# The third FFN's output stage by weight rows, and a mixer that runs two blocks ahead instead of three

## The reference

```python
for i in range(DEPTH):                                     # 2 layers
    sh1, sc1, g1, sh2, sc2, g2, sh3, sc3, g3 = split(silu(c) @ ada_w[i] + ada_b[i], 9)
    x = x + 0.5 * g1 * swiglu_ffn(modulate(rms_norm(x), sh1, sc1), ffn_w_in[i, 0], ffn_w_out[i, 0])
    h = modulate(rms_norm(x), sh2, sc2)
    m = retention(h, ...) if i == 0 else s5_layer(h, ...)  # s5: diagonal scan, then GLU
    x = x + g2 * m
    x = x + 0.5 * g3 * swiglu_ffn(modulate(rms_norm(x), sh3, sc3), ffn_w_in[i, 1], ffn_w_out[i, 1])
return rms_norm(x)

# s5_layer: states = scan(A_bar, u @ B_bar); y = gelu(Re(C states) + d u)
#           y1, y2 = split(y @ w_glu, 2); return y1 * sigmoid(y2)
```

## Time and profile before

| | us |
|---|---|
| median of 3 runs | 2099.3 (2098.71 to 2100.33) |
| span of the profiled execution | 2097.0 |
| TensorE busy in it | 2042.8 (97%) |
| VectorE, ScalarE, GpSimd busy | 1156.3, 602.9, 46.1 |
| output stage of the third FFN | 1447.3 to 1567.0 |
| us_norm | 1567.0 to 1574.0 |
| mixer, first states to last outputs | 1574.0 to 1649.1 |

### The profile page before, as it was taken

The page is one execution under the profiler, slowest core; times in us unless marked ns, Lnnn a source line. Parts: engine busy times, 40 slices in busy tenths (PEclk is TensorE's granted clock), DMA queues, the critical chain, the costliest instruction groups (busy, mean ns, idle before and its releaser), DMA issues.

```text
span 2097.0 us, 26064 instructions
## 1 busy us (share of the span) xinstructions
PE 2042.8 (97%) x10343; PEld 1742.3 (83%) x10343; DVE 1156.3 (55%) x1653; ACT 602.9 (29%) x717; POOL 46.1 (2%) x55
## 2 busy tenths in 40 slices
PE   4999999999999999999999999999998999999998
PEld 3788888988888889888888988888887898888886
DVE  6677556655455436886544566654448664233322
ACT  2322222323323323222222322332332333222222
POOL 2000000000000000000000000000002000000000
PEclk9999999999999999999999999999999999999999
DMA  8465655433132143667545344545668323333221
GB/s 320 140 200 179 201 191 176 136 126 106 61 124 102 45 161 108 213 212 266 171 148 166 114 131 151 162 147 170 203 221 318 116 81 101 100 100 100 90 96 55
DMA packets 246574, 314.89 MB, mean 150 GB/s; under 512 B 31904, under 2 KB 219552, under 8 KB 244128
## 3 DMA queue, kind: packets, MB, share of 16 engines
q1 hardware_dynamic: 212432, 274.74, 39.9%
q10 hardware_dynamic: 34064, 39.07, 5.3%
HBM read 290.44 MB, written 27.53 MB: 152 GB/s over the span
## 4 chain that ended last, share of the span: by engine, by line
PE 60%; issue 32%; DVE 4%; DMA 2%; ACT 1%; POOL 0%; ACTq 0%; POOLq 0%; SPq 0%; DVEq 0%
PE ps L1784 14%; PE ps L1785 14%; PE ps L1786 14%; PE ps L1811 5%; PE ps L1812 5%; PE ps L1815 5%; DVE ada_first L976 1%; DMA sq<-y_dram 1%; PE ps L2070 1%; DMA csil<-in_c 0%; PE ps L2207 0%; DMA y_dram<-acc 0%; DMA tb<-s_lags 0%; PE ps L2061 0%; DVE w_lo L966 0%
## 5 line engine op out<-in xcount | busy, mean ns | idle before, releaser
L550 ACT ACTIVATE w_hi<-w_raw 128x1024 fp32r<-128x1024 f32 x352 | 345.9, 1029 | 350.3 <-PE ps L1786 241.0
L966 DVE TENSOR_TENSOR w_lo<-w_raw,w_hi 128x1024 fp32r<-128x1024 f32 x172 | 210.2, 1222 | 371.7 <-ACT w_hi L550 369.8
L1784 PE MATMUL ps<-g_hi,w_lo 128*128 128x512 f32 (+1 forms) x952 | 345.7, 363 | 0.0
L1786 PE MATMUL ps<-g_hi,w_hi 128*128 128x512 f32 (+1 forms) x952 | 344.9, 362 | 0.0
L1785 PE MATMUL ps<-g_lo,w_hi 128*128 128x512 f32 (+1 forms) x952 | 344.9, 362 | 0.0
L1784 PE MATMUL ps<-h_hi,w_lo 128*128 128x512 f32 x880 | 344.1, 391 | 0.3 <-DVE w_lo L966 0.3
L1786 PE MATMUL ps<-h_hi,w_hi 128*128 128x512 f32 x880 | 342.7, 389 | 0.0
L1785 PE MATMUL ps<-h_lo,w_hi 128*128 128x512 f32 x880 | 342.6, 389 | 0.0
L1811 PE MATMUL ps<-h_hi,w_lo 128*128 128x512 f32 x688 | 269.8, 392 | 2.0 <-DVE w_lo L966 2.0
L1812 PE MATMUL ps<-h_hi,w_hi 128*128 128x512 f32 x688 | 268.5, 390 | 0.0
L1815 PE MATMUL ps<-h_lo,w_hi 128*128 128x512 f32 x688 | 212.4, 390 | 0.0
(11 more groups left out here) (268 smaller groups left out, 2310.1 us busy)
## 6 DMA issues: line engine op xcount, KB each, us to landing
w_raw<-in_ffn_w_in SPq DMA_DIRECT2D x86, 1024.0 KB, 6.2
ada_raw<-in_ada_w SPq DMA_DIRECT2D x128, 512.0 KB, 4.6
w_raw<-in_ffn_w_out SPq DMA_DIRECT2D x32, 1024.0 KB, 6.7
w_raw<-in_ret_w_in SPq DMA_DIRECT2D x24, 1024.0 KB, 5.2
w_raw<-in_ffn_w_out SPq DMA_DIRECT2D x16, 768.0 KB, 4.5
tb<-s_rec ACTq DMA_DIRECT2D x8, 1536.0 KB, 12.5
w_raw<-in_ret_w_out SPq DMA_DIRECT2D x8, 1024.0 KB, 5.1
w_raw<-in_s_w_glu SPq DMA_DIRECT2D x8, 1024.0 KB, 6.2
```

Of the source, the lines that this page charges most:

```text
L550: copy = lambda o, i: nc.scalar.activation(o, i, ACT.Copy)
L966: V.tensor_tensor(w_lo[k % 2][:, 0:HALF, :], w_raw[k % 2][:, 0:HALF, :], raw_f32(w_hi[k % 2][:, 0:HALF, :]), ALU.subtract).then_inc(w_lo_h ...
L1784: nc.tensor.matmul(o, wl, xh, start=start, stop=False)
L1786: return nc.tensor.matmul(o, wh, xh, start=False, stop=stop)
```

## The change

The third FFN's output stage gets functions of its own, `out_by_rows`, on SyncE (written out in `ffn`), ScalarE, VectorE and TensorE. The order of its twelve chunks is now by weight rows: rows 0 to 7 for all four pairs, then rows 8 to 15, then the last six; the eight output tiles are summed in all eight PSUM banks. With that, g's first eight tiles are free after four chunks and the next eight after eight; tables 2 and 3, then 4 and 5, are moved to that space and loaded there during the stage (`tables_in`), tables 0 and 1 behind the second chunk. A modulation half goes with each of the first eight chunks. All residuals and hop stores are in the last four chunks. The last `us_load`s are issued at the start of the mixer. In the mixer states run two blocks ahead on two banks (`AHEAD`), tile 0 of the gelu output is used from block 2 on, a tile per block, and the low part of GLU chunk 1 is made earlier. GpSimd waits for the scans instead of the gelu tiles.

```diff
-V_BANK, Y_BANK = (0, 1, 2, 3, 0, 1, 0, 1), (4, 6, 7, 4, 6, 4, 6, 4)
-Y_HI = ((), (), (0,), (1, 2), (3,), (4,), (5,), (6,))
-Y_USED = ((), (), (), (0,), (1, 2), (3,), (4,), (5,))
+V_BANK, Y_BANK = (0, 1) * 4, (4, 6) * 4
+AHEAD = 2
+Y_HI = ((), (0,), (1,), (2,), (3,), (4,), (5,), (6,))
+Y_USED = ((), (), (0,), (1,), (2,), (3,), (4,), (5,))
...
-        tb += [sb(f"tb{2 + k}", [P, REC], F32, g_at + k * HB) for k in range(4)]
+        tb += [sb(f"tb{2 + k}", [P, REC], F32, (g_at, gl_at)[k % 2] + k // 2 * HB) for k in range(4)]
...
+                if f == 2:
+                    for at in range(len(FFN_OUT) * OUT_PAIRS):
+                        c, o = at // OUT_PAIRS, at % OUT_PAIRS
+                        load(n0 + 2 * FFN_PAIRS + at, at, ffn_out[f][:, 8 * c:8 * c + FFN_OUT[c], o * CW:(o + 1) * CW])
+                        if at < 2 * OUT_PAIRS:
+                            load_ada(a_out + at // 2, *q_of(a_out + at // 2), at % 2)
+                    return
...
-                    elif b < 6:
+                    else:
                         pool.wait_ge(sc_done, b - 2)
-                    else:
-                        pool.wait_ge(a5_lo, (1, 3)[b - 6])
...
+            def out_by_rows(n0, chunks, pair0):
+                for at in range(len(chunks) * OUT_PAIRS):
+                    c, o = at // OUT_PAIRS, at % OUT_PAIRS
+                    split_hi(n0 + at + 1, at + 1, chunks[(at + 1) // OUT_PAIRS % len(chunks)])
+                    if at == 1:
+                        first_tables()
+                    if at in (OUT_PAIRS, 2 * OUT_PAIRS):
+                        act.wait_ge(w_used, n0 + at + 1)
+                        tables_in((2 * c, 2 * c + 1))
+                    if c < len(chunks) - 1:
+                        continue
+                    if o:
+                        for t in range(2):
+                            us_load(2 * o - 2 + t)
+                    square(pair0 + o, 2 * o)
+                    if o == OUT_PAIRS - 1:
+                        split_hi(C_GLU + 1, 1)
+                    if o == 0:
+                        act.wait_ge(scale_u, 1)
+                    for t in range(2):
+                        u_tile(2 * o + t)
...
-                for r in range(2):
-                    act.wait_ge(u_out[r], 16 * KT // 2)
-                tables_in(range(2, 6))
+                for t in range(KT - 2, KT):
+                    us_load(t)
...
-                    if b == 0:
+                    if b == 1:
                         act.wait_ge(w_lo_done, C_GLU + 3)
                         tables_in(range(6, KT))
-                    if b == 1:
-                        for t in range(KT - 2, KT):
-                            us_load(t)
...
+                split_lo_half(C_GLU + 1, 1)
                 dve.wait_ge(rstd_done, k + 1)
...
-                split_lo_half(C_GLU + 1, 1)
+                split_lo_rest(C_GLU + 1, 1)
...
+            def out_by_rows(n0, chunks, pair0, ada):
+                for at in range(len(chunks) * OUT_PAIRS):
+                    c, o = at // OUT_PAIRS, at % OUT_PAIRS
+                    split_lo(n0 + at + 1, at + 1, chunks[(at + 1) // OUT_PAIRS % len(chunks)])
+                    if at < 2 * OUT_PAIRS:
+                        ada_half(ada + at // 2, at % 2)
+                    if c < len(chunks) - 1:
+                        continue
+                    pair = pair0 + o
+                    dve.wait_ge(tile_done, pair - TILES_LESS[pair0 // OUT_PAIRS])
+                    residual_of(2 * o, 2 * o).then_inc(x_half, 1)
...
+            def out_by_rows(n0, chunks, g_all):
+                pe.wait_ge(win_copied, KT)
+                pe.wait_ge(lag_copied, KT)
+                pe.wait_ge(skip_added, KT)
+                for c, r in enumerate(chunks):
+                    if c == len(chunks) - 1:
+                        pe.wait_ge(g_lo_done, g_all)
+                    for o in range(OUT_PAIRS):
+                        at = c * OUT_PAIRS + o
+                        if c == len(chunks) - 1:
+                            chunk_by_tile(n0 + at, at, g_hi, g_lo, 8 * c, r, 2 * o, False, tile_done)
+                        else:
+                            chunk(n0 + at, at, g_hi, g_lo, 8 * c, r, 2 * o, c == 0, False)
...
-                for b in range(3):
+                for b in range(AHEAD):
                     states(b)
                     chunk_outputs(b)
...
                     outputs(b)
-                    if b == 3:
+                    if b + AHEAD < KT:
+                        states(b + AHEAD)
+                    if b == AHEAD:
                         pe.wait_ge(w_lo_done, C_GLU + 3)
-                        pe.wait_ge(gelu_done, 3)
                     for done in Y_USED[b]:
                         first_glu(done)
-                    if b + 3 < KT:
-                        states(b + 3)
-                    if b < 2:
-                        chunk_outputs(b + 3)
-                    elif 3 <= b < KT - 2:
-                        chunk_outputs(b + 2)
+                    if b + AHEAD < KT:
+                        chunk_outputs(b + AHEAD)
```

106 lines of the change are left out of this document (56 added, 50 removed).

## The result

The changed kernel takes 2133.38 us (median of 4 runs, 2132.45 to 2135.55) where the kernel before takes 2099.01 (4 runs, 2097.84 to 2100.33): a ratio of 1.0167, 95% interval 1.0152 to 1.0181. The sign of the forecast was right and its size was not: +34.4 us instead of +23.0, and 2133.4 lies above the range of 2108 to 2130.

What follows compares the result with a forecast made beforehand. TensorE's own work was taken to bound the kernel, so only its waits could move the time. The stage's +27.0 us and the mixer's -4.0 gave +23.0 on 2099.3, so 2122.3 us, with a range of 2108 to 2130.

Steps and rivals of the forecast that it cites:

- The bound: Whole kernel: TensorE's work bounds it, so only its waits move time; stage has none to lose, mixer 9.5 us.
- The loading loop: Output stage, SyncE's queue: weights load singly, 13.9 us per loop against a turn of 10.9; stage loses 26.3 us.
- six waits: TensorE idle ahead of w_lo between 1480 and 1561: 3 us each, 6 to 8 at chunks 3 and 6, some 26.
- The bandwidth: Loads behind tables: 406 GB/s taken; at 358 GB/s two chunks land some 2 us later each, sum 4 us higher.
- The last four turns: End of output stage: VectorE's and ScalarE's work both under 8.2 us per turn, so no cost; 0.7 added for clock.
- The norm: Ahead of the mixer's first states: a 0.3 us delay from the earlier GLU low half, counted within the mixer's sum.
- The mixer: Waits fall from 11.2 to 7.0 us with the new order and early tables; gain 4 us, from 1.5 to 6.
- (c): Mixer gains nothing, as block 1's y travels with tables 6 and 7 and scans wait; 2126.3 us, chance 0.13.
- (a): Output stage: tables pass in the weight queue's pauses, chunks 3 and 6 after 13.9 us; 2111.9 us, chance 0.14.
- (b): Output stage: weights keep up, stage stays at 119.7 us, only the mixer's gain left; 2095.3 us, chance 0.06.
- (d): Effects cancel: larger lead and shorter landings, so the stage loses only 4 to 8 us; 2099 to 2103, chance 0.03.
- VectorE's gap of 4 us: Mixer: VectorE's long idle of 4.39 us, while ScalarE waited for block 0's y, was to be gone afterwards.

Runs made afterwards that it cites:

- E1: Changed kernel with each modulation half in SyncE's queue moved behind the next weight load; 2104.4 us, ratio 1.0026.
- e2: Changed kernel with VectorE doing each modulation half ahead of the split of the next chunk, SyncE's queue unchanged; 2105.5 us, ratio 1.0036.
- E7: E1 with ScalarE's last four turns reordered: high split, one hop copy, first square, other copy, second square; 2097.1 us, ratio 0.9990 to the kernel before.
- e11: Changed kernel with only E7's ScalarE order in the last four turns, SyncE's queue unchanged; 2128.3 us, ratio 1.0140.
- e8: E1 with all eight hop copies and their loads moved behind the stage's last square and last high split; 2106.8 us, one run.
- e6: New mixer alone: changed kernel with the earlier kernel's output stage and tables 2 to 5 loaded at the mixer's start; 2106.8 us, ratio 1.0043.
- E10: E7 with GpSimd's scaling for blocks 5 to 7 waiting for VectorE's low half of the gelu output; 2095.4 us, ratio 0.9986.
- e12: E7 with ScalarE's gelu high halves and the GLU products at their old, later blocks, states still two blocks ahead; 2094.5 us, ratio 0.9981.
- e13: e12 with GpSimd's multiply also waiting for VectorE's gelu low half, as in the kernel before; 2094.3 us, ratio 0.9978.

## Why the prediction was right in sign and short in size

**The bound.** That only TensorE's waits can move the time, and that the stage had none to lose, held but for the clock: 10343 matmuls in both, and all differences are waits or clock. Of the 36.2 us 14.1 are slower matmuls and 22.1 are waits, and the sum had priced the clock at 0.7.

**The loading loop** was right in mechanism. The chunks were forecast for 1486.3, 1500.2, 1514.1, 1533.2, 1547.1 and 1560.6 and came at 1486.3, 1501.2, 1516.1, 1534.3, 1548.9 and 1562.8. The period is 14.9 us instead of 13.9. The part from landing to next issue is 14.9 - 8.6 = 6.3 us (6.6 in the forecast), so the miss is the landing: 8.6 us where the nearest rows, 7.0 and 7.7, made me take 7.3. Chunk 3, behind tables 0 and 1, came to the tenth as forecast, because the landing was longer (13.2 instead of 12.5) and the steps around it shorter; the turn behind tables 2 and 3 took 18.2 us (1516.1 to 1534.3) instead of 19.1. In sum chunk 8 came 2.2 us later than forecast. E1 and e2 show the loop as the cause. I forecast six waits of 3 and 6 to 8 us; they are 1.8 to 6.7, 21.4 in sum, and the other 7 us up to chunk 8 are products at a low clock (0.92 in the window), which start TensorE's next turn later and so shorten its next wait. I had named that and counted it once, which came out right.

**The bandwidth.** A window of the kernel before, with the tables of the mixer under way, moves 427 GB/s, and the two landings behind tables, 13.2 and 11.9 us, are on average what I had put (12.5):

```profile
1580.00:1585.00 5.00, 4.22 (x38) 4.12 (x38) 4.72 (x6) 1.59 (x2) 1.48 (x2) 1.00 1.01 427
```

The 358 GB/s per core of the Trainium skill, "DMA: Bandwidth & Descriptors", section "Specifications", would by the estimate in the prediction have made the sum 4 us higher, with some 2 us more at each of these two landings. These rows speak against it; that the measured time lies nearer to that sum has another cause, the next one.

**The last four turns** are the step that failed. "Both under 8.2, so nothing" compares sums of busy time with the turn. These turns cost 7.7 us, 7.0 more than the 0.7 I had added for the clock. The two engines hand one piece to each other and back twice per turn, and a chain of handovers over two in-order queues took 9.8 us with neither of them full. E7 and e11 show that it is this order, and e8 that the copies can't simply go. With the loop kept and this order mended (e11) the kernel takes 2128.3 us, which is inside the range.

**The norm** was in no term of the sum but for 0.3 us. It took 2.2 more: TensorE came to it from a wait of 4.8 us and ran it at 0.50, where the kernel before has 0.75 in the same stretch and e7, without that wait, 1.00. That the wait is the reason is not shown: e11 has waits of only 1.0 and 1.3 us there and the norm still took 9.2.

**The mixer.** The gain of 4 (1.5 to 6) was meant from the norm on, and there only 0.1 us was gained: 2.3 in the mixer, 2.2 lost in the norm. So this term was 3.9 us too good. The 2.3 us also came for another reason than my count. The collision of block 0's y with 12 MB of tables was the true cost, as said, and the early tables remove it (75.1 to 68.7 us in the old order). But I credited TensorE's shorter waits with two blocks ahead as part of the same gain; in e6 and e7 the new order takes instead of giving. E10, e12 and e13 lay that on the earlier use of the gelu output and on GpSimd's new rule, and not on the two blocks. Rival (c) was half right: block 1's y travels with tables 6 and 7 and ScalarE stands 6.3 us (changed kernel, at 1647.17) to 7.85 us (e7) for it.

The three misses, 2.3 us up to chunk 8, 7.0 in the last turns and 3.9 from the norm on, are the 13.2 us between the 36.2 of the traces and the 23.0 of the sum.

**Rivals.** (a) and (b) are excluded: the turn behind tables was 3.2 us longer than the others, and no 1 MB landing of the stage was under 7.9 us. (b)'s condition holds in e1, where the loads run ahead of the turns (loads at 1480.3 and 1487.7, 7.5 us apart), and its 2095.3 is near to e7's 2097.1, where ScalarE's order is mended as well. (d) is excluded too: the stage lost 28.6 us up to chunk 8, not 4 to 8. Of the signs I had named, the single loads and the six waits are there and VectorE's gap of 4 us is gone; a seventh wait, 1.44 us at chunk 11, was not foretold.

**The range.** It allowed 4 us above the forecast for the landings and 2.5 for the mixer, and nothing for a cost where I had written "nothing". The last four turns alone took 7.0 of the 7.7 us between the forecast and the upper bound.

## What to carry to other kernels

Two engines that hand a piece back and forth need the length of the chain over both of them, from one square to the next, compared with the turn; the sum of each one's work does not tell it. In a queue that issues in order, a transfer that waits for a late consumer makes the transfers behind it single, so put such a one behind the urgent load, or let the consumer read it first. Where two delays lie side by side, taking one away shows little (1.3 and 1.5 us here, against 4.5 for both): take both before calling either harmless.
